# The weight-block sums of two feed-forward layers on GpSimd instead of VectorE

## The reference, cut to what matters

```python
h = modulate_2(x, g_mlp[i], sh2, sc2)
y = jnp.square(jax.nn.relu(h @ w_ff1[i])) @ w_ff2[i]
x = x + gt2[:, None, :] * y
```

## Time and profile before

| | |
|---|---|
| median of 3 runs | 3029.17 us |
| the runs | 3027.86, 3029.17, 3033.00 us |
| the profiled execution, its span | 3027.7 us |
| around the span, to the fastest run and to the median | 0.2 us, 1.5 us |
| TensorE busy | 2908.8 us, 96% |
| VectorE busy | 1656.7 us, 55% |
| ScalarE busy | 722.1 us, 24% |
| GpSimd busy | 71.7 us, 2% |
| mean granted TensorE clock | 0.991 |

### The profile page before, as it was taken

One profiled execution on the slowest core, in us unless ns is written; L12 is line 12 of the kernel. 1 busy time (PEld: TensorE's weight loads), 2 busy tenths in 40 slices (PEclk: granted clock), 3 DMA queues, 4 the chain that ended last, 5 costly groups with the idle time before them and its releaser, 6 DMA issues.

```text
span 3027.7 us, 36246 instructions
## 1 busy us (share of the span) xinstructions
PE 2908.8 (96%) x14418; PEld 2184.0 (72%) x14418; DVE 1656.7 (55%) x2729; ACT 722.1 (24%) x1393; POOL 71.7 (2%) x136
## 2 busy tenths in 40 slices
PE   7999999999899999989999999999999998999998
PEld 5988888788557888844444434478888846888887
DVE  4777887365666677621111157464555467655545
ACT  4444444220672001111011022420000116200001
POOL 0000000000000111000000001000000020000000
PEclk9999999999999999999999999999999999999999
DMA  5100111021103555379999967012222270122221
GB/s 236 70 36 35 65 41 56 35 91 56 67 12 104 211 184 219 118 326 421 422 422 422 422 265 319 28 56 84 84 84 84 112 279 29 56 84 93 101 85 56
DMA packets 71751, 451.73 MB, mean 149 GB/s; under 512 B 8032, under 2 KB 10224, under 8 KB 24112
## 3 DMA queue, kind: packets, MB, share of 16 engines
q1 hardware_dynamic: 53840, 374.17, 30.9%
q0 software_dynamic: 17040, 73.18, 6.7%
q10 hardware_dynamic: 720, 2.29, 0.2%
HBM read 445.41 MB, written 2.10 MB: 148 GB/s over the span
## 4 chain that ended last, share of the span: by engine, by line
PE 85%; DVE 8%; DVEq 2%; DMA 2%; ACT 2%; issue 1%; ACTq 0%; SPq 0%
PE PS L253 78%; PE PS L1671 1%; PE PS L1556 1%; PE PS L1654 1%; DVE arena L1621 1%; DVE stat L1680 1%; DVEq L1124 1%; DMA hT<-stream 1%; PE PS L2451 1%; DMA ring<-stream 1%; DMA arena<-x 1%; PE PS L2431 1%; ACT arena L1574 0%; DVE arena L1120 0%; DVE PS L2782 0%
## 5 line engine op out<-in xcount | busy, mean ns | idle before, releaser
L253 PE MATMUL PS<-arena 128*128 128x256 f32 (+3 forms) x4960 | 982.6, 388 | 17.0 <-DVE arena L1162 8.5
L253 PEld LDWEIGHTS PS<-arena 128*128 128x128 f32 (+1 forms) x4960 | 742.8, 183 | 232.4 <-issue 146.9
L253 PE MATMUL PS<-arena,ring 128*128 128x256 f32 (+1 forms) x1992 | 466.9, 390 | 0.0
L253 PEld LDWEIGHTS PS<-arena,ring 128*128 128x128 f32 x1992 | 377.8, 190 | 73.8 <-issue 25.5
L253 PE MATMUL PS<-hT,ring 128*128 128x256 f32 (+1 forms) x1504 | 400.6, 421 | 7.2 <-ACT hT L420 6.2
L253 PEld LDWEIGHTS PS<-hT,ring 128*128 128x128 f32 x1504 | 284.4, 190 | 110.5 <-issue 77.9
L253 PE MATMUL PS<-xT,arena 128*128 128x256 f32 x1056 | 232.4, 379 | 0.0
L253 PEld LDWEIGHTS PS<-xT,arena 128*128 128x128 f32 x1056 | 200.5, 190 | 31.5 <-issue 4.8
L2203 DVE TENSOR_TENSOR arena<-arena,PS 128x512 f32<-128x512 f32 x16 | 11.0, 687 | 370.1 <-PE PS L253 370.1
L253 PE MATMUL PS<-hT,arena 128*128 128x256 f32 (+1 forms) x864 | 195.1, 442 | 0.8 <-DMA hT<-stream 0.8
L597 DVE CUSTOM_DVE_ANT_0 arena<-arena,PS 128x1024 f32<-128x1024 f32 x128 | 152.1, 1217 | 43.0 <-DMA arena<-adat 41.2
(11 more groups left out here) (312 smaller groups left out, 3018.3 us busy)
## 6 DMA issues: line engine op xcount, KB each, us to landing
ring<-stream SPq DMA_DIRECT2D x217, 1024.0 KB, 7.1
arena<-stream SPq DMA_DIRECT2D x98, 1024.0 KB, 18.3
arena<-adat POOLq DMA_DIRECT2D x88, 512.0 KB, 4.9
hT<-stream SPq DMA_DIRECT2D x32, 1024.0 KB, 18.7
arena<-adat POOLq DMA_DIRECT2D x20, 1024.0 KB, 10.8
arena<-stream SPq DMA_DIRECT2D x8, 512.0 KB, 4.4
arena<-x ACTq DMA_DIRECT2D x4, 512.0 KB, 15.3
xT<-stream SPq DMA_DIRECT2D x2, 1024.0 KB, 20.9
```

The costliest lines, as they stand in the source:

```text
L253: ins = nc.tensor.matmul(out_, lhsT, rhs, start=start, stop=stop_, **kw)
```

## The change

`weight_sums` is given to GpSimd. It works out its own unit number, waits as before for both units of the quad, and then for the last reader of the buffer it writes: the first projection quad's products for a layer's quad 0, product 1 of quad 0 for quad 1, and for later quads all products up to quad `q - 2`. Its four instructions have the same operands, order and semaphore counts. GpSimd's queue gets the sums of quads 0 to 14 of the first layer ahead of its wait for quad 13, those of quad 15 behind the four tile issues that follow it, and those of the second layer behind the remaining transfers. The calls in VectorE's queue and the argument `before_last` go.

```diff
--- before.py
+++ after.py
@@ -1857,7 +1857,7 @@
                 squares_early(act, use, n - n0, 0, (p_c, n + 1))
             scales_early(act, use, 0)
 
-        def residual_dve(v, n0, gate, tmp, use, ready=None, before_last=None):
+        def residual_dve(v, n0, gate, tmp, use, ready=None):
             for n in (n0, n0 + 1):
                 part = n - n0
                 x_ = halves_of(xT, 4 * part)
@@ -1870,8 +1870,6 @@
                                                              ALU.mult, ALU.add)
                     ins.then_inc(done, 1)
 
-                if part and before_last is not None:
-                    before_last()
                 last_sum_dve(v, n)
                 if part:
                     first_sums(v, use, 0)
@@ -2547,17 +2545,25 @@
             act.wait_ge(q_p, 7 * q + 2)
             nc.scalar.activation(Xc[:, q % 2, 1, :, :], bank_of(q, 1), ACT.Copy).then_inc(q_x, 1)
 
-        def weight_sums(v, q, u):
+        def weight_sums(pool, q):
+
+            u = U_FF[q // QF] + 2 * (q % QF)
             A = weight_blocks(u)
             S = Sw[:, q % 2, :, :, :]
-            unit_wait(v, u)
-            unit_wait(v, u + 1)
-            nc.vector.tensor_tensor(S[:, 0, :, :], A[1, 0], A[1, 1], ALU.add).then_inc(q_s, 1)
-            nc.vector.tensor_tensor(S[:, 2, :, :], A[0, 0], A[1, 0], ALU.subtract).then_inc(q_s, 1)
-            v.drain()
-            nc.vector.tensor_tensor(S[:, 1, :, :], S[:, 0, :, :], A[0, 0], ALU.subtract).then_inc(q_s, 1)
-            v.drain()
-            nc.vector.tensor_tensor(S[:, 3, :, :], A[0, 1], S[:, 1, :, :], ALU.subtract).then_inc(q_s, 1)
+            unit_wait(pool, u)
+            unit_wait(pool, u + 1)
+            if q % QF == 0:
+                pool.wait_ge(p_p, 7 * ((N_MWO, N_SWO)[q // QF] + 1))
+            elif q % QF == 1:
+                pool.wait_ge(q_p, 7 * (q - 1) + 1)
+            else:
+                pool.wait_ge(q_p, 7 * (q - 1))
+            nc.gpsimd.tensor_tensor(S[:, 0, :, :], A[1, 0], A[1, 1], ALU.add).then_inc(q_s, 1)
+            nc.gpsimd.tensor_tensor(S[:, 2, :, :], A[0, 0], A[1, 0], ALU.subtract).then_inc(q_s, 1)
+            pool.drain()
+            nc.gpsimd.tensor_tensor(S[:, 1, :, :], S[:, 0, :, :], A[0, 0], ALU.subtract).then_inc(q_s, 1)
+            pool.drain()
+            nc.gpsimd.tensor_tensor(S[:, 3, :, :], A[0, 1], S[:, 1, :, :], ALU.subtract).then_inc(q_s, 1)
 
         def moving_sums(v, X, Tt, ready=None):
             B = halves(X, 1)
@@ -2661,15 +2667,13 @@
 
         def ff_dve(v, L, use):
             for n, (kind, kc, part) in enumerate(FF_ORDER):
-                q, u = QF * L + n, U_FF[L] + 2 * n
+                q = QF * L + n
                 if n == 0:
                     moving_sums(v, hT, T_h, NM[use])
                 if n == QF - 1:
                     first_sums(v, use + 1, 1)
                 quad_mid(v, q)
-                if n + 1 < QF:
-                    weight_sums(v, q + 1, u + 2)
-                elif L == 0:
+                if n == QF - 1 and L == 0:
                     mod_diag(v, 3)
                 v.drain()
                 if kind == 1:
@@ -2874,12 +2878,17 @@
             pool.dma_start(posi, pos).then_inc(in_pool, 16)
             pool.wait_ge(e_ys, 2 * NPAIR + 1)
             tiles(56, 96)
+            for q in range(QF - 1):
+                weight_sums(pool, q)
             pool.wait_ge(q_p, 7 * 14)
             tiles(96, 100)
+            weight_sums(pool, QF - 1)
             pool.wait_ge(x_ok, 4)
             pool.dma_start(bvs, bv).then_inc(in_pool, 16)
             pool.dma_start(snk[:, 0, :], sinks).then_inc(in_pool, 16)
             tiles(100, 128)
+            for q in range(QF, 2 * QF):
+                weight_sums(pool, q)
 
         @block.tensor
         def _(pe):
@@ -2955,8 +2964,7 @@
             sums_dve(v, N_MWO)
             v.wait_ge(mla_out, 8)
             block_sums(v, qn, T_w)
-            residual_dve(v, N_MWO, lambda j: mod2[:, 16 + j:17 + j], Vq, 7,
-                         before_last=lambda: weight_sums(v, 0, U_FF[0]))
+            residual_dve(v, N_MWO, lambda j: mod2[:, 16 + j:17 + j], Vq, 7)
             norm_halves(v, 7)
             ff_dve(v, 0, 7)
             norm_dve(v, 8, xT, hT)
@@ -2965,8 +2973,7 @@
             sums_dve(v, N_SWO)
             v.wait_ge(swa_out, 8)
             block_sums(v, qn, T_w)
-            residual_dve(v, N_SWO, lambda j: mod2[:, 64 + j:65 + j], Vq, 9,
-                         before_last=lambda: weight_sums(v, QF, U_FF[1]))
+            residual_dve(v, N_SWO, lambda j: mod2[:, 64 + j:65 + j], Vq, 9)
             norm_halves(v, 9)
             ff_dve(v, 1, 9)
             end_dve(v)
```

## The result

The changed kernel is slower: 3037.20 us (median of 15 runs, 3035.83 to 3039.72) against 3032.93 us for the kernel before in the same comparison (15 runs, 3027.76 to 3035.49). The ratio is 1.0017, with a 95% interval of 1.0009 to 1.0024, so 5.2 us (2.7 to 7.3); the two medians lie 4.3 us apart. The kernel before is 3.8 us slower here than in the three runs that the prediction started from, which are among the 15.

What follows compares the result with a forecast made beforehand. TensorE's matmul time was taken to bound the kernel; 0 (removed) + 0 (steady) + 0 (projection) + 0.65 us (layer starts), added to the median of 3029.17, gave 3029.8 us, with a range of 3026 to 3036.

Steps and rivals of the forecast that it cites:

- What bounds the kernel: Whole kernel: TensorE is busy 96% of 3027.7 us and throughout each 24.2 us quad, so only matmul time counts.
- the removal: VectorE, 32 quads: four sums fewer per quad, 156 us of busy time, none on the path; cost 0.
- the steady quads: Feed-forward quads after the start: GpSimd's sums cost nothing for d up to 6.0 us; cost 0.
- GpSimd's duration: One 128x1024 sum on GpSimd: taken as 2.45 us, twice VectorE's row, within 1.22 to 6.0.
- the projection: Before each layer: four quad-0 sums end by 2020.5, or 2026.9 if VectorE's reads are shared; cost 0.
- its point of delay: End of the projection: VectorE's first piece that TensorE can't do without a delay, last-corner gating, is at 2027.88.
- The first rival: Layer starts: GpSimd and VectorE wait for each other's reads and the cover runs out; 5.9 us to +15; chance 0.10.
- point of decision: Layer starts: the slower case was to set in at about d = 3.0, with 2.95 us a layer, 5.9 us.
- d: GpSimd's duration of one 128x1024 sum, taken as 2.45 us.
- The layer's start: Quad 1's sums beside VectorE's moving sums in quad 0: 0 to +1.3 us for both layers, taken as 0.65.
- The sums of quad 15: Last quad of the first layer: its GpSimd sums were to end 15 us before product 2 of quad 15.
- the tail of the first rival: Projection's end at d = 4.0: the fourth sum holds VectorE's normalisation until 2033.1, about 3.75 us.

Runs made afterwards that it cites:

- e7: On top of e3, each sum of quads 2 to 15 of both layers is made twice on GpSimd; ratio 1.0003 to the kernel before.
- e8: On top of e3, each sum of quads 2 to 15 of both layers is made three times on GpSimd; 3219.45 us in a single execution.
- e3: The changed kernel with GpSimd's drains between the sums replaced by waits on the semaphore that the sums raise; ratio 1.0002 to the kernel before.
- e5: The changed kernel with one more GpSimd drain in each layer, behind its last transfers and ahead of the quad-0 sums; ratio 1.0003 to the kernel before.

## Why the prediction was wrong

*What bounds the kernel, the removal, the steady quads*: right. TensorE had no gap in a quad before or after, the removed 156 us gave nothing, and e7 and e8 put the break between 4 x 2 and 4 x 3 sums a quad: 86% of GpSimd at no cost, and a pace set by it above.

*GpSimd's duration*: taken as 2.45 us, measured as 2.35 alone and 2.4 to 2.6 in the means of a line, up to 3.4 where VectorE holds it up. By an estimate from the 4497 ns for 2048 columns of the Trainium skill, page "GPSIMD Engine Reference", section 3.1, it would be 2.25; the trace is 0.1 us above that.

*The step that failed* is the projection: "Four of them take 9.8 us at 2.45, to 2020.5 ... so an end by 2026.9 ... Cost 0". The sums were laid end to end, and the drains between them put at nothing without a reason; all that the prediction says of them is "The instruction counts match one to one, drains included". Behind 98 transfers the first of them cost 8.19 us, and so the third and fourth sum came at 2020.79 and 2023.30, with VectorE at its additions for the last corners. Counted from product 2 of the projection's second quad (2006.19 before, 2002.69 after), the forecast end of the sums is 14.3 to 20.7 us and its point of delay 21.7 us. They ended at 23.0 us in the changed kernel, and at 15.4 us in e3. e3 and e5 take away the pause alone and the loss goes with it.

The piece that came late was not the one that the prediction named, the gating of the last corner at 2027.88, but the sum of squares before it (L375, at 2026.01 in the profile after), which is what TensorE's new wait names.

*The first rival* had the mechanism, that the two engines keep each other waiting in the start, and the wrong point of decision. It asked for a d of 3.0; at 2.35 to 2.8 the pause did it. Its chance of 0.10 was too low because it hung on d alone. In the trace an instruction of VectorE with two SBUF inputs waits for the whole GpSimd sum (0.68 became 2.83 us), while additions with one input in PSUM kept their time (0.67 at 2018.01 in e3, with GpSimd's third sum beside them). The Trainium skill's page "SBUF — State Buffer", section "Who interferes with whom", says that instructions of the first kind contend with a GpSimd instruction that reads SBUF and those of the second don't. The trace agrees.

The blocking also explains most of VectorE's 115 us in place of 156: instructions that are held up count as busy. Compared one by one with the profile before, those beside a GpSimd sum are 33.7 us longer in total, and the others are as long as they were.

*The layer's start*, priced at 0 to 1.3 us, cost nothing: in e3 VectorE's third and fourth moving sums took 6.50 us together in place of 2.54, and TensorE ran through products 2 to 4 of quad 0 without a gap:

```profile
2038.68 10.52 PE L253 MATMUL PS<-arena 128*128 128x256 f32 x48
```

*Two readings* were off without changing the forecast. The sums of quad 15 were to end 15 us before product 2 of that quad; by the prediction's own figures (units landed at 2380, 9.8 us of sums, product 2 at 2399.8) it is 10 us, and in the changed kernel it was 7.4. And the tail of the first rival at a d of 4.0, about 3.75 us, doesn't follow from its row: 2033.1 less 2027.88 is 5.2.

*The range* was missed for a second reason: it was set on three runs with a median of 3029.17, and 15 runs of the kernel before gave 3032.93. With 5.2 us on top of 3029.17 it would have held. The clock in the starts can be part of that spread: a stretch was 1.6 to 1.7 us longer each time it fell in the profiles of before.

## What to carry to other kernels

Where arithmetic moves to GpSimd and GpSimd also issues transfers, the first drain behind them pays 0.082 to 0.085 us for each; put one in idle time ahead (e5), or wait on the instruction's own semaphore (e3). Where work moves off a busy engine onto one that shares its operand reads, look at the few microseconds in which that engine is on the path, and not at its mean. A moved part that hides under TensorE gave nothing here, however much busy time it freed: with the pause removed, the change is no faster than the kernel before (1.0002 and 1.0003), and no version here beats it.

## What the runs showed of the hardware

A drain on GpSimd takes, on top of 0.16 us, 0.082 to 0.085 us for each transfer that the engine has issued since its drain before, even though the last of them had been issued about 130 us earlier in the first layer. What the engine does in that time was not tried and stays open. And TensorE's granted clock may or may not fall to 0.50 after the same idle time: 3.11 us ahead of product 1 left it at 1.00 in one profile of the kernel before and took it to 0.50 in another. In the first layer it held in seven of the eight profiles with a mean granted clock of 0.90 from 1950 to 2000 us, and fell in all five with 0.93 or 0.97. Why it does so is open, and so is what decides in the second layer.
